# Layer norm of the convolution taken along rows: statistics for each token by bn_stats, rows transposed in and out of PSUM

## The reference

```python
def layernorm(x, gain, bias):
    xf = x.astype(jnp.float32)
    mu = jnp.mean(xf, axis=-1, keepdims=True)
    var = jnp.mean(jnp.square(xf - mu), axis=-1, keepdims=True)
    y = (xf - mu) * lax.rsqrt(var + LN_EPS)
    return (y * gain.astype(jnp.float32) + bias.astype(jnp.float32)).astype(x.dtype)

def conv_module(a_hist, c_in, conv_w, conv_b, ln_g, ln_b, conv_pw):
    a, g = jnp.split(c_in, 2, axis=-1)
    a = a * jax.nn.sigmoid(g)
    full = jnp.concatenate([a_hist, a], axis=1)
    ...
    y = lax.conv_general_dilated(full, conv_w[:, None, :], ...) + conv_b
    y = jax.nn.silu(layernorm(y, ln_g, ln_b))
    return y @ conv_pw, full[:, -CONV_HIST:]
```

## Time and profile before

| | us |
|---|---|
| median of three runs | 1161.32 |
| lowest and highest run | 1161.10, 1161.77 |
| the profiled execution | 1161.36 |
| its span, first to last instruction | 1159.3 |
| TensorE busy in the span | 1148.5 (99%) |
| GpSimd busy | 806.0 (70%) |
| VectorE busy | 598.5 (52%) |
| ScalarE busy | 532.8 (46%) |

### The profile page before, as it was taken

The page is one execution under the profiler, slowest core; times in us unless marked ns, Lnnn a source line. Parts: engine busy times, 40 slices in busy tenths (PEclk is TensorE's granted clock), DMA queues, the critical chain, the costliest instruction groups (busy, mean ns, idle before and its releaser), DMA issues.

```text
span 1159.3 us, 22766 instructions
## 1 busy us (share of the span) xinstructions
PE 1148.5 (99%) x7914; PEld 1132.1 (98%) x7914; DVE 598.5 (52%) x878; ACT 532.8 (46%) x801; POOL 806.0 (70%) x421
## 2 busy tenths in 40 slices
PE   7999999999999999999999999999999999999999
PEld 6999999999899999999999999999998999999998
DVE  5865562239967544432258655522598764444100
ACT  5444444444765444444444444444457654444332
POOL 6776667777776766667667766677786776666674
DMA  8444445557535544445565444455573654443453
GB/s 295 153 162 146 145 118 149 149 171 221 159 120 165 173 146 154 143 122 148 159 196 161 147 146 146 119 149 162 179 211 114 183 154 153 152 152 124 138 149 107
DMA packets 72203, 180.91 MB, mean 156 GB/s; under 512 B 10210, under 2 KB 25826, under 8 KB 72162
## 3 DMA queue, kind: packets, MB, share of 16 engines
q1 hardware_dynamic: 71680, 179.23, 49.8%
q10 hardware_dynamic: 482, 1.16, 0.3%
HBM read 176.78 MB, written 3.58 MB: 156 GB/s over the span
## 4 chain that ended last, share of the span: by engine, by line
PE 96%; DMA 1%; DVE 1%; ACT 1%; POOL 0%; issue 0%; SPq 0%; DVEq 0%
PE bank L611 28%; PE bank L614 28%; PE bank L612 28%; PE bank L897 2%; PE bank L899 2%; PE bank L898 2%; PE bank L671 1%; PE bank L672 1%; PE bank L670 1%; DMA x<-in_xT 1%; DMA raw<-in_w 0%; PE bank L879 0%; PE bank L857 0%; PE bank L732 0%; PE bank L839 0%; POOL w_lo L506 0%
## 5 line engine op out<-in xcount | busy, mean ns | idle before, releaser
L506 POOL TENSOR_TENSOR w_lo<-raw,w_hi 128x1024 fp32r<-128x1024 f32 (+2 forms) x351 | 766.5, 2189 | 321.0 <-ACT w_hi L985 320.5
L985 ACT ACTIVATE w_hi<-raw 128x1024 fp32r<-128x1024 f32 (+2 forms) x351 | 336.5, 961 | 439.2 <-PE bank L614 423.2
L611 PE MATMUL bank<-xg_hi,w_hi 128*128 128x320 f32 x1552 | 481.8, 310 | 0.9 <-DVE tmp L1264 0.9
L614 PE MATMUL bank<-xg_hi,w_lo 128*128 128x320 f32 x1552 | 479.6, 309 | 0.0
L612 PE MATMUL bank<-xg_lo,w_hi 128*128 128x320 f32 x1552 | 479.5, 309 | 0.0
L611 PEld LDWEIGHTS bank<-xg_hi,w_hi 128*128 128x128 f32 x1552 | 291.3, 188 | 3.7 <-issue 1.9
L612 PEld LDWEIGHTS bank<-xg_lo,w_hi 128*128 128x128 f32 x1552 | 291.4, 188 | 0.4
L614 PEld LDWEIGHTS bank<-xg_hi,w_lo 128*128 128x128 f32 x1552 | 291.3, 188 | 0.0
L611 PE MATMUL bank<-h_hi,w_hi 128*128 128x320 f32 x704 | 217.5, 309 | 0.0
L612 PE MATMUL bank<-h_lo,w_hi 128*128 128x320 f32 x704 | 217.5, 309 | 0.0
L614 PE MATMUL bank<-h_hi,w_lo 128*128 128x320 f32 x704 | 217.5, 309 | 0.0
(11 more groups left out here) (188 smaller groups left out, 816.6 us busy)
## 6 DMA issues: line engine op xcount, KB each, us to landing
raw<-in_w SPq DMA_DIRECT2D x223, 512.0 KB, 3.8
raw<-in_w SPq DMA_DIRECT2D x64, 384.0 KB, 3.0
raw<-in_w SPq DMA_DIRECT2D x64, 320.0 KB, 2.9
k_all<-in_cache_kT SPq DMA_DIRECT2D x32, 128.0 KB, 3.5
v_past<-in_cache_v SPq DMA_DIRECT2D x32, 128.0 KB, 2.8
cst<-in_consts ACTq DMA_DIRECT2D x1, 997.0 KB
out_yT<-x SPq DMA_DIRECT2D x1, 960.0 KB, 4.9
x<-in_xT SPq DMA_DIRECT2D x2, 320.0 KB, 3.8
```

What stands on the lines that cost most here:

```text
L506: pool.tensor_tensor(w_lo[:, j, 0:count * P], raw[:, j, 0:count * P], w_hi[:, j, 0:count * P].bitcast(F32), ALU.subtract).then_inc(split.s ...
L611: pe.matmul(out, hi, in_hi[:, k, :], start=first and n == 0, stop=False)
L614: mm = pe.matmul(out, lo, in_hi[:, k, :], start=False, stop=last and end)
L985: act.activation(w_hi[:, j, 0:count * P], raw[:, j, 0:count * P], ACT.Copy).then_inc(split_hi.sem, 1)
```

## The change

The two sums by a matrix of ones, the subtraction, the squares, the 320-column reciprocal and the multiplication go. TensorE transposes conv_y so that tokens lie on partitions: the 256 prompt tokens into bank 7 (`conv_rows`), the 64 sample tokens into bank 1 (`conv_sample_rows`). VectorE copies the sample rows to SBUF, takes bn_stats over the 256 channels of each token and bn_aggr (mean and variance), ScalarE takes the root of the variances (three columns), VectorE inverts it and writes the normalised rows (subtract, multiply). `conv_columns` transposes them back (prompt to bank 7, sample to bank 4), and ScalarE applies gain, bias and Silu from there, prompt and sample apart. Beside that, the copy of v_tok on ScalarE moves ahead of the squares of the gate, the second take_pool on VectorE moves behind the bn_stats, prob_new waits for the last projection column itself, and `batch_attention_transposes` changes places with `pool_map`.

```diff
             def sample_rows(L):
 
-                hold(pe, v_copied.sem, v_copied.at(L, 1))
+                hold(pe, cv_stat.sem, cv_stat.at(L, 1))
...
-            def conv_mean(L):
+            def conv_rows(L):
                 pe.wait_ge(taps.sem, taps.at(L, taps.per))
+                for c in range(GT):
+                    for t in range(2):
+                        mm = pe.transpose(bank[7][:, t * 2 * P + c * P:t * 2 * P + (c + 1) * P], conv_y[:, c, t * P:(t + 1) * P], ident)
+                mm.then_inc(cv_tr.sem, 1)
+
+            def conv_sample_rows(L):
+
                 pe.wait_ge(late_taps.sem, late_taps.at(L, late_taps.per))
-                for c in range(GT):
-                    mm = pe.matmul(bank[7][:, 0:TOK], ones[:, :], conv_y[:, c, :], start=c == 0, stop=c == 1)
-                mm.then_inc(cv_mean.sem, 1)
-
-            def conv_variance(L):
-                pe.wait_ge(cv_sq.sem, cv_sq.at(L, 2))
-                for c in range(GT):
-                    mm = pe.matmul(bank[7][:, 0:TOK], ones[:, :], conv_sq[:, c, :], start=c == 0, stop=c == 1)
-                mm.then_inc(cv_var.sem, 1)
+                pe.wait_ge(v_copied.sem, v_copied.at(L, 1))
+                for c in range(GT):
+                    mm = pe.transpose(bank[1][0:NS, c * P:(c + 1) * P], conv_y[:, c, SEQ:TOK], ident)
+                mm.then_inc(cv_tr.sem, 1)
+
+            def conv_columns(L):
+
+                pe.wait_ge(cv_ln.sem, cv_ln.at(L, 3))
+                for c in range(GT):
+                    for t in range(2):
+                        mm = pe.transpose(bank[7][:, c * SEQ + t * P:c * SEQ + (t + 1) * P],
+                                          conv_tok[:, t * 2 * P + c * P:t * 2 * P + (c + 1) * P], ident)
+                mm.then_inc(cv_back.sem, 1)
+                pe.wait_ge(mix_ok.sem, mix_ok.at(L, 3))
+                for c in range(GT):
+                    mm = pe.transpose(bank[4][:, c * NS:(c + 1) * NS], conv_tok_s[:, c * P:(c + 1) * P], ident[0:NS, 0:NS])
+                mm.then_inc(cv_back.sem, 1)
...
-                pe.wait_ge(cv_act.sem, cv_act.at(L, 2))
+                pe.wait_ge(cv_act.sem, cv_act.at(L, 4))
...
-                conv_mean(L)
+                conv_rows(L)
                 value_rows(L)
                 column(L, BASE_I, T_I, 3, 3)
-                conv_variance(L)
+                conv_sample_rows(L)
...
                 batch_attention(L)
+                conv_columns(L)
                 open_outputs(L, {6: 1, 7: 2}, first=True)
                 conv_map(L)
+                batch_attention_transposes(L)
                 pool_map(L)
-                batch_attention_transposes(L)
...
+                act.wait_ge(cv_stat.sem, cv_stat.at(L, 7))
+                act.activation(norm_stat[:, 24:27], norm_vars, ACT.Sqrt, bias=eps_ln, scale=1.0).then_inc(cv_rt.sem, 1)
...
                 for c in range(GT):
-                    hold(act, cv_ln.sem, cv_ln.at(L, c + 2))
-                    act.activation(conv_y[:, c, :], conv_y[:, c, :], ACT.Silu, scale=vec[:, bass.ds(L * NV + (V_LG + c), 1)],
+                    hold(act, cv_back.sem, cv_back.at(L, 1))
+                    act.activation(conv_y[:, c, 0:SEQ], bank[7][:, c * SEQ:(c + 1) * SEQ], ACT.Silu, scale=vec[:, bass.ds(L * NV + (V_LG + c), 1)],
+                                   bias=vec[:, bass.ds(L * NV + (V_LB + c), 1)]).then_inc(cv_act.sem, 1)
+                for c in range(GT):
+                    hold(act, cv_back.sem, cv_back.at(L, 2))
+                    act.activation(conv_y[:, c, SEQ:TOK], bank[4][:, c * NS:(c + 1) * NS], ACT.Silu, scale=vec[:, bass.ds(L * NV + (V_LG + c), 1)],
...
                 take_pool(0)
-                dve.wait_ge(cv_mean.sem, cv_mean.at(L, 1))
-                for c in range(GT):
-                    dve.scalar_tensor_tensor(out=conv_y[:, c, :], in0=bank[7][:, 0:TOK], scalar=-1.0 / (GT * P), in1=conv_y[:, c, :],
-                                             op0=ALU.mult, op1=ALU.add).then_inc(cv_cent.sem, 1)
...
-                take_pool(1)
...
+                dve.wait_ge(slots.sem, slots.at(L, 4 * BASE_I + 16))
...
-                dve.wait_ge(cv_rt.sem, cv_rt.at(L, 1))
-                dve.reciprocal(bank[7][:, 0:TOK], conv_root[:, :]).then_inc(cv_ln.sem, 1)
+                dve.wait_ge(cv_tr.sem, cv_tr.at(L, 2))
+                dve.tensor_copy(conv_tok_s, bank[1][0:NS, 0:GT * P]).then_inc(cv_stat.sem, 1)
+                dve.wait_ge(cv_stat.sem, cv_stat.at(L, 1))
+                dve.bn_stats(norm_stat[0:NS, 12:18], conv_tok_s).then_inc(cv_stat.sem, 1)
+                for t in range(2):
+                    dve.bn_stats(norm_stat[:, 6 * t:6 * t + 6], bank[7][:, t * GT * P:(t + 1) * GT * P]).then_inc(cv_stat.sem, 1)
+                take_pool(1)
+                dve.wait_ge(cv_stat.sem, cv_stat.at(L, 4))
+                for t in range(3):
+                    n = P if t < 2 else NS
+                    dve.bn_aggr(norm_stat[0:n, 18 + 2 * t:20 + 2 * t], norm_stat[0:n, 6 * t:6 * t + 6]).then_inc(cv_stat.sem, 1)
...
+                dve.wait_ge(cv_rt.sem, cv_rt.at(L, 1))
+                dve.reciprocal(norm_stat[:, 28:31], norm_stat[:, 24:27]).then_inc(cv_inv.sem, 1)
+                dve.wait_ge(cv_inv.sem, cv_inv.at(L, 1))
+                for t in range(3):
+                    n = P if t < 2 else NS
+                    out = conv_tok[:, t * GT * P:(t + 1) * GT * P] if t < 2 else conv_tok_s
+                    src = bank[7][:, t * GT * P:(t + 1) * GT * P] if t < 2 else conv_tok_s
+                    dve.tensor_scalar(out, src, norm_stat[0:n, 18 + 2 * t:19 + 2 * t], norm_stat[0:n, 28 + t:29 + t],
+                                      ALU.subtract, ALU.mult).then_inc(cv_ln.sem, 1)
                 gate_low(0)
-                dve.wait_ge(cv_ln.sem, cv_ln.at(L, 1))
-                for c in range(GT):
-                    dve.tensor_tensor(conv_y[:, c, :], conv_y[:, c, :], bank[7][:, 0:TOK], ALU.mult).then_inc(cv_ln.sem, 1)
                 gate_low(1)
```

More of the change, by code:

```diff
@@ L156, in hybrid_decoder @@
         stat = sb("stat", [P, 64])
+        norm_stat = sb("norm_stat", [P, 32])
         prob = sb("prob", [P, HEADS, 3 * P])
@@ L203, in hybrid_decoder @@
         gm_squares = tmp[:, 2, 0:GT * P]
-        conv_sq = tmp[:, 0:2, :]
-        conv_root = tmp[:, 3, :]
+        conv_tok = tmp[:, 0:2, :].rearrange("p c t -> p (c t)")
+        conv_tok_s = tmp[0:NS, 3, 0:GT * P]
+        norm_means, norm_vars = norm_stat[:, 18:24:2], norm_stat[:, 19:24:2]
         at, views, const_at = 0, {}, {}
@@ L304, in hybrid_decoder @@
         pool_hi = sig("pool_hi", 2)
[L305 to L308, removed]
+        cv_tr = sig("cv_tr", 2)
+        cv_stat = sig("cv_stat", 7)
         cv_rt = sig("cv_rt", 1)
+        cv_inv = sig("cv_inv", 1)
         cv_ln = sig("cv_ln", 3)
-        cv_act = sig("cv_act", 2)
+        cv_back = sig("cv_back", 2)
+        cv_act = sig("cv_act", 4)
         cv_pw = sig("cv_pw", 2)
@@ L1149, in _ @@
                                    accum_out=stat[:, 36 + g:37 + g]).then_inc(s_exp.sem, 1)
+                act.wait_ge(v_tr.sem, v_tr.at(L, 1))
+                act.activation(v_tok[:, :, :].rearrange("p t n -> p (t n)"), bank[1][:, :], ACT.Copy).then_inc(v_copied.sem, 1)
                 act.wait_ge(gm_tr.sem, gm_tr.at(L, 2))
@@ L1157, in _ @@
                     act.activation(gm_squares[rows, :], src, ACT.Square, accum_out=stat[rows, 40 + t:41 + t]).then_inc(gm_sq_ok.sem, 1)
-                act.wait_ge(v_tr.sem, v_tr.at(L, 1))
-                act.activation(v_tok[:, :, :].rearrange("p t n -> p (t n)"), bank[1][:, :], ACT.Copy).then_inc(v_copied.sem, 1)
-                for c in range(GT):
-                    act.wait_ge(cv_cent.sem, cv_cent.at(L, c + 1))
-                    act.activation(conv_sq[:, c, :], conv_y[:, c, :], ACT.Square).then_inc(cv_sq.sem, 1)
                 act.wait_ge(gm_sq_ok.sem, gm_sq_ok.at(L, 3))
                 act.activation(stat[:, 44:47], stat[:, 40:43], ACT.Sqrt, bias=eps_rms, scale=1.0 / (GT * P)).then_inc(gm_rt.sem, 1)
-                act.wait_ge(cv_var.sem, cv_var.at(L, 1))
-                act.activation(conv_root[:, :], bank[7][:, 0:TOK], ACT.Sqrt, bias=eps_ln, scale=1.0 / (GT * P)).then_inc(cv_rt.sem, 1)
                 act.wait_ge(gm_inv.sem, gm_inv.at(L, 1))
@@ L1230, in _ @@
                 last = dve.memset(ap, value)
+            last = dve.memset(norm_stat[:, :], 1.0)
             last.then_inc(filled.sem, 1)
```

## The result

The kernel after takes 1171.08 us in the median of five runs (1169.33 to 1172.41), against 1161.32 us (1161.1 to 1162.02) for five runs of the kernel before: the ratio is 1.0081, with a 95% interval of 1.007 to 1.0093. The forecast was 1167.8 with a range of 1164.7 to 1172.0. It is slower, as forecast, and by 3.3 us more than forecast. (Where the runs of a kernel spread, the ratio given with an interval is not just the quotient of the medians.)

A forecast was written before the change was run, and what follows sets the result against it. TensorE, busy for 99% of the span, was taken as the bound. A late take (1.25 us) and the transposes back (1.94) make 3.2 us a layer, 6.4 in two: 1161.4 + 6.4 = 1167.8 us, range 1164.7 to 1172.0.

The forecast's parts named there:

- TensorE's own work: TensorE in the mixer: sums of 2.28 us go, twelve transposes of 1.3 us come, about 1.0 us a layer gained.
- The wait: TensorE ahead of the sample probabilities: stands 2.9 us for the late second take_pool, starting them 1.25 us later.
- The walk along VectorE: VectorE from 307.06 us, instruction by instruction through prob_new, copy and three bn_stats, to the take's end at 314.2.
- the other reading: prob_new on VectorE: about 0.25 us instead of 0.85 if GpSimd is idle then, 0.6 us a layer less.
- The way back: Normalised rows transposed back, table load and four Silu ahead of the pointwise map: 1.94 us more a layer.
- The second hole ahead of the map: TensorE ahead of the pointwise map: a hole of 0.5 to 1.3 us, released by the Silu.
- Edits with no price: Remaining edits, such as the reciprocal removed, new root, pool_map exchange and GpSimd's later window sums: no cost expected.
- The clock: TensorE's clock in the new stall: a fall to the 1.2 GHz level was given only chance 0.06.
- a sign that the prediction named itself: TensorE behind the hole: the forecast is wrong if matmuls there take twice as long.
- rival 4: TensorE's clock falls in the new stall: 2.8 us a layer more, 1173.4 us; chance 0.06.
- rival 3: Heavier statistics on VectorE: bn_stats at 0.80 us and a scaling waiting for GpSimd, 4.8 a layer, 1171.0 us; chance 0.12.
- The sum of the forecast: Whole kernel: 3.2 us a layer slower, 6.4 us in two layers, 1167.8 us.

The follow-up runs named there:

- take_early: The changed kernel with the second take_pool moved back to its old place, behind the small reciprocal; 1163.88 us, ratio 1.0021.
- late_take_alone: The kernel before with only its second take_pool moved late, behind the 320-column reciprocal; 1166.54 us, ratio 1.0054.
- way_back_covered: The changed kernel with the second take_pool back early, Silu's table loaded early and sample columns transposed into free bank 2; 1161.36 us, ratio 1.0.
- stand_longer: The kernel before with the second take_pool moved late and one unused 128x320 multiplication ahead of it; 1170.03 us, ratio 1.0071.
- gap_filled: The changed kernel with 24 extra unused transposes a layer ahead of the prompt's last four; 1167.76 us, ratio 1.0057.

## Why the prediction was right, and where it was not

- **TensorE's own work.** Forecast: 1.0 us a layer less, and arrival at line 806's successor at 311.3. Measured: the last transpose ahead of the stand ends at 312.40, less the late start of 0.96 that is 311.44. Right.
- **The wait.** Forecast: 1.25 us a layer, behind a stand of 2.9 us. Measured: 1.18 in both layers, behind 2.68 and 2.69. The walk along VectorE held in its steps: the product ahead of prob_new took 1.26 us instead of 0.92, but it ended together with ScalarE's root, which the next instruction needs anyway (311.29 less the late start, forecast 311.2); prob_new ends at 312.18 once the late start is taken off (forecast 312.1), and copy, three statistics and take go from 313.06 to 315.03, 1.97 us instead of 2.1. The run take_early shows that the order, not the amount of work on VectorE, made the stand. That prob_new would keep its length was a choice between two readings, and the row (0.76 us, ending 0.16 behind a GpSimd add of 311.79 to 312.98) is near the one taken; the other reading, about 0.25, is what late_take_alone shows with GpSimd idle (0.28).
- **The way back.** Forecast: 1.94 us a layer (its terms as written add up to 1.92). Measured: 1.95 and 1.96. Part of the match is luck: in layer 0 the four Silu took 1.61 us instead of 1.80, and the handing over 0.26 instead of 0.1. The second hole ahead of the map is 0.69 us in layer 0, ended by Silu, within the 0.5 to 1.3 that were named. In layer 1 the same total is made of another wait (0.74 ahead of the sample columns, since the scaling of the sample rows ran into GpSimd's product; 0.28 more, ahead of line 799, falls into the middle piece): what is late there takes the place of the wait for Silu. The run way_back_covered shows that at full clock 1.09 of it were waits; the rest is TensorE's work and the restart around it.
- **Edits with no price.** GpSimd's fourth add starts at 315.11 (314.15 without the late start; forecast 314.3), the pooling map at 329.84 follows the transposes ahead of it without a bracket, and what follows the map is within 0.1 us of before. Right.
- **The clock.** This is the step that failed, and by a sign that the prediction named itself: matmuls behind the hole taking twice as long. From the start of line 823's four transposes to the next row's start it is 0.91 us (315.09 to 316.00), where it was 0.44 before (312.95 to 313.39). The argument against rival 4 was that the new gap is less than half of the one at the start of the program, and that TensorE is busy until it. Both are true, and neither excluded the fall: the clock fell in both layers of the profiled run. Its price was set at 2.8 us a layer, from a guess that the low level would last as long as at the start. Measured: 1.57 in layer 0 and 1.69 in layer 1 (1.97 less the wait of 0.28), where the low level lasted 3.4 us; 3.08 where it lasted 6.8, in stand_longer. Across runs it differs: against the 1167.8 us of full clock, after's five runs lie 1.5 to 4.6 us higher. The case had 0.06 of the chance and was what happened. The result lies in the range only because the range reached out to rival 3, heavier statistics, and that one did not occur (0.40 us each); so far that is luck.

The sum of the forecast, 6.4 us, is what the change costs at full clock: gap_filled gives 1167.76 less 1161.39, 6.37 us. Most of that price is waits of TensorE: with them covered (way_back_covered) it is gone. The 3.3 us on top, in the median, are the clock's.

## What to carry to other kernels

- Before statistics or any other work are put into the queue of an engine that also frees PSUM banks, look which bank's release stands behind them: TensorE stood 2.7 us for a take of half a microsecond, and moving that one line back regained 7.2 of 9.8 us.
- A stand of TensorE like those here (2.0 to 2.7 us) is to be priced twice: as the delay itself, and as what the stream behind it may cost at 1.2 GHz (1.6 to 3.1 us where the clock fell). Look at the granted clock behind each hole, and at the scatter of the runs, which can be a sign of it.
- Removing one wait tells little where another is due right behind it, or while another disturbance is still there. With the late take and the lower clock, loading Silu's table early moved the median by nothing that could be told; with the take early, the table and the freed bank together gave 1.09 us a layer. What the table gives alone was not run there.

## What the hardware showed that was not expected

- The granted clock fell to 0.50 after stands of 2.68 and 2.69 us in the profiled run of after, at the end of the stand, for some 3.4 us. After the same stand of 2.4 us it stayed at 1.00 in one layer of a run and fell in the next, there a microsecond after TensorE had resumed and for 6.8 us. With a stand of 2.0 us a whole profiled run kept 1.00, and another run of the same kernel had a mean of 0.996 and took 5 us more.
- Filling a hole with 24 useless transposes made the kernel 3.3 us faster.
- A tensor_scalar of 64x256 that reads and writes SBUF took 0.39 us alone and 1.31 to 1.38 us beside a GpSimd product of 128x512; with its input in PSUM, 128x256 took 0.54 us in both layers, but not beside that product.
- A product of 128x128 with both inputs in SBUF (prob_new) took 0.28 us with GpSimd idle, and 0.76 to 0.85 us where a GpSimd add that reads SBUF ran into it.
- A bn_stats over 256 columns took 0.40 us from PSUM, no longer than a product that reads 128x256 from PSUM (line 1408, 0.40), and a bn_aggr 0.14 us.
